# Seven-product pairs begun at pair 6 in the feed-forward entries, and conditioning units moved out of them

## The chip, the cores and the metric

The kernel runs on one core of a Trainium2 chip. The time is the device time of one execution in microseconds (us). Three runs of the kernel before gave 2658.09, 2658.15 and 2658.76 us (median 2658.15 us).

TensorE multiplies matrices and writes PSUM; VectorE (DVE in the rows) and ScalarE (ACT) do elementwise work; GpSimd (POOL) does elementwise work and issues some of the DMAs; the queue of SyncE (SP) issues the weight loads.

## The reference, cut to what matters

One inference step of a two-layer encoder over 576 tokens: 512 of a prompt and 64 of a sample, each group with a conditioning vector of its own. Per layer:

```
h += 1/2 * gate1 * RMSNorm(SwiGLU(mod1(RMSNorm(h))))     feed-forward "a"
x  = mod2(RMSNorm(h)); three mixers and a gated merge;  h += gate2 * RMSNorm(m @ W_out)
h += 1/2 * gate3 * RMSNorm(SwiGLU(mod3(RMSNorm(h))))     feed-forward "b"

swiglu(x, w1, w2): g, u = split(x @ w1); return (silu(g) * u) @ w2      x 576x1024, w1 1024x5504
mod, gate:         silu(c) @ w_ada + b_ada        9 vectors of 1024 for each layer and group
```

All of it is float32. The change touches the product `x @ w1` (four times: layers 0 and 1, "a" and "b") and the place in the program of a part of `silu(c) @ w_ada`.

## The kernel before, in words

**Products.** Activations lie transposed: features on the 128 partitions, the 576 tokens in two halves of 288 columns. Each float32 weight tile and each activation is split into a high part (a cast on ScalarE) and a low part (raw minus high, on VectorE), and a product is three matmuls: high x high, high weight x low activation, low weight x high activation. Weights come in chunks of 128x1024 in a ring of five slots (`SLOTS`), loaded by SyncE's queue when the chunk that had the slot five chunks earlier has been read (`load`). `split_hi` (line 1483) and `split_lo` (line 2004) make `w_hi` and `w_lo` of a chunk.

**A feed-forward entry.** The 5504 columns of `w1` are taken as 21 pairs (a gate tile and an up tile of 128 columns) and a half pair. A plain pair is two chunks, each 8 tiles x 3 matmuls x 2 halves, so 96 matmuls of 128x288. Pairs 0 to 4 (`NORMED = 5`) run on activations that lack the norm factor and the shift; beside them ScalarE and VectorE make the finished activation `x_full`, and the last of these pairs is followed by casting it into `x_hi` (line 1624) and subtracting to `x_lo` (line 2222). Pair 5 reads these tile by tile (`x_is_full`), pair 6 is plain too.

**Seven-product pairs.** Pairs 7 to 12 (`JOIN0, JOIN1 = 7, 13`) use Strassen's scheme in Winograd's form: gate and up tiles, the two halves of the rows and the two halves of the tokens make a 2x2 block product, done in seven block products instead of eight. That is 7 parts x 4 tiles x 3 = 84 matmuls of 128x288 (`joined_pair`; its matmuls are line 935). It needs sums of activations, `t_raw` (`t_sums`: four GpSimd instructions, lines 2911 to 2915, high parts at 1497, low parts at 2021), once for an entry, and sums of weights, `w_raw` (`sum_of_w`: four GpSimd instructions for a pair, called orders 0 to 3 here, line 2901; high parts 1492, low parts 2014), for each pair. TensorE reads a pair's weights as four chunks v = 0 to 3, and waits for the low part of each before parts 0, 2, 4 and 6. The low part of v = 0 stands behind order 1, those of v = 1, 2 and 3 behind order 3. VectorE adds the seven results up (line 2055).

Order 0 needs the loaded chunk v = 0, order 1 the chunk v = 1, order 2 the end of the chunk that holds the slot of v = 3, order 3 the chunk v = 2.

**Conditioning units.** A unit is one 128x512 piece of `w_ada`: a GpSimd-issued DMA into `ada_w`, and two VectorE instructions (line 2112) that multiply it by the conditioning of either group and sum along the row. `ADA_STAGES` says which stage computes which vectors, `f1_units`, `f2_units` and `gate_units` how many units VectorE does at each place. In layer 0's entry "a" alone, one unit stands in each seven-product pair, and GpSimd issues its next load between the pairs' weight sums.

The order of work on every engine is written out by hand. ScalarE, VectorE and GpSimd each run their list in that order.

Of the kernel before, what the change touches and what calls it, by code (L numbers as in the profile page):

```python
# [12 lines left out]
P = 128  # L13
# [3 lines left out]
TOK = SEQ + DEC  # L17
# [54 lines left out]
JOIN0, JOIN1 = 7, 13  # L72
# [19 lines left out]
ADA_STAGES = [((0, "f1a"), (2, 4, 3), (2, 4)), ((0, "f2a"), (3, 5, 7), (5, 7)), ((0, "gate"), (6,), (6,)),  # L92
# [37 lines left out]
def f1_units(l, ab, i):  # L130

    if (l, ab) == (1, "b"):
        return 2 if i >= JOIN1 else 0
    if (l, ab) == (0, "a"):
        return 1 if JOIN0 <= i < JOIN1 else {13: 5, 14: 5, 15: 6, 17: 5, 18: 5, 19: 4, 20: 4}.get(i, 0)
    return {13: 5, 14: 5, 15: 6, 17: 4, 18: 4, 19: 4, 20: 4}.get(i, 0)
# [20 lines left out]
def gate_units(m):  # L157

    return {1: (1, 1), 2: (1, 2), 3: (1, 2), 5: (1, 1), 6: (1, 2), 7: (1, 2)}.get(m, (0, 0))
# [258 lines left out]
def build_program(nc, ins, outs):  # L418
# [68 lines left out]
    ada_junk = sb("ada_junk", [P, ADA_K], at=big + JOIN1 * TOK * 4)  # L487
# [979 lines left out]
    def _(act):  # L1467
# [62 lines left out]
        def ffn_up(l, ab):  # L1530
# [12 lines left out]
            for i in range(NORMED):  # L1543
# [6 lines left out]
                else:  # L1550
                    for k in range(KD):
                        high_of_full(l, ab, k)
                        if k in (2, 5):
                            split_hi()
# [16 lines left out]
                elif i == 3:  # L1571
                    split_hi()
            for i in range(NORMED, KF - 1):
# [5 lines left out]
                if i == JOIN0 - 1:  # L1579
# [4 lines left out]
                if i == NORMED:  # L1584
                    high_of_t(l, ab, 2, 0)
                    high_of_t(l, ab, 1, 1)
                act.wait_ge(chunk_done.sem, chunk_done.done(0, chunk(l, ph, f1_chunk(i))))
                A(two(sil[:, i, :]), pair[0], ACT.Silu).then_inc(acc_free[0].sem, 1)
                if i == NORMED:
                    high_of_t(l, ab, 3, 2)  # L1590
                    high_of_t(l, ab, 0, 3)
                if i == JOIN0 - 1:
# [3 lines left out]
                if i > NORMED:  # L1596
                    split_hi()
# [385 lines left out]
    def _(dve):  # L1983
# [87 lines left out]
        def joined_stage(l, ab, i):  # L2071
# [22 lines left out]
            ada(l, "f1" + ab, f1_units(l, ab, i), ada_junk[:, :])  # L2094
# [7 lines left out]
        def ada(l, ph, n, junk=None):  # L2102

            for u in range(modulated[0], min(modulated[0] + n, ADA_ENDS[l, ph])):
# [4 lines left out]
                for g in (0, 1):  # L2109
                    so_far = ada_all[:, at, g:g + 1]  # L2110
                    out = ada_w[:, u % 2, :] if g else junk or ada_out[u % 2]
# [8 lines left out]
        def ffn_up(l, ab):  # L2120
# [4 lines left out]
            for i in range(NORMED):  # L2125
# [24 lines left out]
                else:  # L2150
                    for k in range(KD):
                        low_of_full(l, ab, k)
                        if k in (2, 5):
# [20 lines left out]
            for i in range(NORMED, KF - 1):  # L2174
# [3 lines left out]
                if i == NORMED:  # L2178
                    split_lo()
                    low_of_t(l, ab, 0)  # L2180
                    low_of_t(l, ab, 1)
                elif i == JOIN0 - 1:
                    low_of_t(l, ab, 2)
                    low_of_t(l, ab, 3)
                    low_of_joined(l, ab, JOIN0, 0)
# [10 lines left out]
                elif i > NORMED:  # L2196
# [571 lines left out]
        def merge(l):  # L2768
            for m in range(KD):
                g0, g1 = GROUP_AT["gate"]  # L2770
                for br, s in enumerate((0, 1, 0)):
                    if m or br == 2:
                        split_lo()
                    if br:
                        ada(l, "gate", gate_units(m)[br - 1])
# [87 lines left out]
    def _(pool):  # L2863
# [53 lines left out]
        def sums_and_loads(l, ab):  # L2917
# [249 lines left out]
```

## Time and profile before

| | |
|---|---|
| median of three runs | 2658.15 us |
| the profiled execution's own time | 2657.02 us |
| its span in the profile | 2655.3 us |
| TensorE busy | 2613.1 us, 98% of the span |
| VectorE busy | 1729.9 us, 65% |
| ScalarE busy | 1059.9 us, 40% |
| GpSimd busy | 393.8 us, 15% |
| granted TensorE clock, mean | 0.997 |

Busy times say how long an engine had work; a busy VectorE instruction can also be one that stands waiting inside itself, which only its length against others of its shape shows. The chain of waits is followed back from the last instruction, and shows which engine each stretch of time belongs to.

### The profile page before, as it was taken

Reading aid. Unit: us, or ns where it says so; the run is one execution under the profiler, and the core shown is the slowest. Engines: PE = TensorE matmul, PEld = TensorE weight load, DVE = VectorE, ACT = ScalarE, POOL = GpSimd, SP = SyncE. Lnnn points to the kernel's source line nnn. Section 1 sums busy time; section 2 is a strip of 40 time slices with the busy share of each in tenths; the row PEclk is TensorE's granted clock in tenths of the full one; section 3 lists DMA queues with packets and bytes.
Section 4 is the critical chain, followed back from the end, with each engine's and each line's share of the span. In section 5 each row is a group of like instructions: output and inputs, shape, how many; then the busy total and the mean of one; then the engine's idle time right before and its main releaser. Section 6 shows DMA issues by size and latency. Waiting matters only on the chain.

```text
span 2655.3 us, 49061 instructions
## 1 busy us (share of the span) xinstructions
PE 2613.1 (98%) x20410; PEld 2526.7 (95%) x20410; DVE 1729.9 (65%) x3490; ACT 1059.9 (40%) x1912; POOL 393.8 (15%) x484
## 2 busy tenths in 40 slices
PE   7999999999999999999999999999999999999997
PEld 6989999888999999999999999998889999999997
DVE  5797777766656487777487776576666565875423
ACT  4542224544422474322265322254452335542321
POOL 0341120110000013211104211101100000240000
PEclk9999999999999999999999999999999999999998
DMA  6245554443333323455423455534333332244321
GB/s 263 85 148 169 185 186 135 128 131 102 96 113 106 93 71 116 152 174 175 132 88 100 147 187 162 159 104 138 115 110 100 110 109 80 72 139 133 111 88 60
DMA packets 105997, 336.84 MB, mean 127 GB/s; under 512 B 15084, under 2 KB 18732, under 8 KB 105072
## 3 DMA queue, kind: packets, MB, share of 16 engines
q1 hardware_dynamic: 75376, 233.26, 27.0%
q0 software_dynamic: 30400, 100.45, 12.1%
q8 instruction: 161, 2.64, 0.4%
q14 instruction: 60, 0.49, 0.1%
HBM read 322.76 MB, written 11.55 MB: 126 GB/s over the span
## 4 chain that ended last, share of the span: by engine, by line
PE 92%; DVE 4%; issue 1%; DMA 1%; POOL 1%; ACT 0%; DVEq 0%; SPq 0%; ACTq 0%
PE ps L879 77%; PE ps L935 8%; PE ps L1318 2%; PE ps L1366 1%; PE ps L1342 1%; DMA ada_first<-in_ada_first 1%; DVE w_lo L2004 1%; PE ps L888 1%; POOL w_raw L2901 1%; DVE x_lo L2222 0%; DVE w_lo L2014 0%; PE ps L1335 0%; PE ps L997 0%; DVE hid L2161 0%; DVE prob L2677 0%
## 5 line engine op out<-in xcount | busy, mean ns | idle before, releaser
L879 PE MATMUL ps<-x_hi,w_hi 128*128 128x288 f32 (+1 forms) x3456 | 777.1, 299 | 4.3 <-DVE x_lo L2222 1.5
L879 PE MATMUL ps<-x_hi,w_lo 128*128 128x288 f32 (+1 forms) x3456 | 759.5, 294 | 0.0
L879 PE MATMUL ps<-x_lo,w_hi 128*128 128x288 f32 (+1 forms) x3456 | 759.5, 294 | 0.0
L879 PEld LDWEIGHTS ps<-x_hi,w_hi 128*128 128x128 f32 x3456 | 558.6, 188 | 18.0 <-issue 8.5
L879 PEld LDWEIGHTS ps<-x_lo,w_hi 128*128 128x128 f32 x3456 | 561.5, 188 | 0.3
L879 PEld LDWEIGHTS ps<-x_hi,w_lo 128*128 128x128 f32 x3456 | 561.5, 188 | 0.0
L2004 DVE TENSOR_TENSOR w_lo<-w_raw,w_hi 128x1024 fp32r<-128x1024 f32 x336 | 418.9, 1250 | 138.7 <-ACT w_hi L1483 136.2
L1483 ACT CAST w_hi<-w_raw 128x1024 fp32r<-128x1024 f32 x336 | 348.5, 1048 | 79.3 <-DMA w_raw<-in_f 78.6
L879 PE MATMUL ps<-hid_hi,w_hi 128*128 128x288 f32 x1344 | 301.1, 295 | 0.0
L879 PE MATMUL ps<-hid_lo,w_hi 128*128 128x288 f32 x1344 | 299.4, 293 | 0.0
L879 PE MATMUL ps<-hid_hi,w_lo 128*128 128x288 f32 x1344 | 299.0, 294 | 0.0
L2867 POOL DMA_DIRECT2D ada_w<-in_ada x256 | 137.9, 539 | 978.2 <-DVE ada_all L2112 965.4
L2112 DVE CUSTOM_DVE_ANT_0 ps<-ada_w,c_half,ada_all 128x512 f32<-128x512 f32 x250 | 189.0, 756 | 127.9 <-DMA ada_w<-in_ada 127.4
L879 PEld LDWEIGHTS ps<-hid_hi,w_hi 128*128 128x128 f32 x1344 | 219.8, 188 | 0.2
L879 PEld LDWEIGHTS ps<-hid_lo,w_hi 128*128 128x128 f32 x1344 | 219.4, 188 | 0.2
L879 PEld LDWEIGHTS ps<-hid_hi,w_lo 128*128 128x128 f32 x1344 | 217.2, 187 | 0.0
L2112 DVE CUSTOM_DVE_ANT_0 ada_w<-ada_w,c_half,ada_all 128x512 f32<-128x512 f32 x256 | 191.2, 747 | 0.0
L2901 POOL TENSOR_TENSOR w_raw<-w_raw 128x512 f32<-128x512 f32 x96 | 147.7, 1549 | 191.8 <-DMA w_raw<-in_f 113.5
L1656 ACT ACTIVATE sq<-ps 128x576 f32<-128x576 f32 x38 | 24.9, 655 | 294.5 <-PE ps L888 261.5
L2014 DVE TENSOR_TENSOR w_lo<-w_raw,w_hi 128x1024 fp32r<-128x1024 f32 x96 | 115.4, 1205 | 26.6 <-POOL w_raw L2901 26.6
L2243 DVE TENSOR_TENSOR acc_y<-acc_y,sq 128x576 f32<-128x576 f32 (+1 forms) x51 | 32.9, 644 | 142.5 <-ACT sq L1656 116.5
L1935 ACT ACTIVATE sig<-sig,z 128x512 f32<-128x512 f32 x96 | 46.0, 528 | 185.3 <-DVE z L2779 185.2
(279 smaller groups left out, 3805.5 us busy)
## 6 DMA issues: line engine op xcount, KB each, us to landing
w_raw<-in_f SPq DMA_DIRECT2D x236, 512.0 KB, 3.6
ada_w<-in_ada POOLq DMA_DIRECT2D x256, 256.0 KB, 3.3
w_raw<-in_gate SPq DMA_DIRECT2D x64, 512.0 KB, 3.7
w_raw<-in_f SPq DMA_DIRECT2D x92, 256.0 KB, 2.7
w_raw<-in_tri SPq DMA_DIRECT2D x40, 512.0 KB, 3.6
ada_first<-in_ada_first SPq DMA_DIRECT2D x4, 2048.0 KB, 21.3
w_raw<-in_wout SPq DMA_DIRECT2D x16, 512.0 KB, 3.6
c_half<-c_scratch POOLq DMA_DIRECT2D x12, 512.0 KB, 5.5
```

Source lines behind the costliest of these rows:

```text
L879: r = mm(ps[:, 2 * out + b, 0:width], w, xx[:, cols(b)], start=first and n == 0, stop=last and n == 2)
L888: r = mm(ps[:, 2 * out + b, 0:HALF], w[:, s, t * P:(t + 1) * P], hid_hi[:, k, columns(b)], start=False, stop=w is w_lo)
L935: r = mm(ps[:, bank, 0:HALF], w, moved, start=k == 0 and m == 0, stop=k == half_k - 1 and m == 2)
L1318: r = mm(out, q_st[rows, i * P:i * P + m], k, start=True, stop=True)
L1483: copy(w_hi[:, c % SLOTS, :], w_in[:, c % SLOTS, :]).then_inc(hi_ready.sem, 1)
L1935: r = A(sig[:, br, part], sig[:, br, part], ACT.Sigmoid, bias=c_col[:, br, g:g + 1])
L2004: V.tensor_tensor(w_lo[:, s, :], w_in[:, s, :], w_hi[:, s, :], ALU.subtract).then_inc(lo_ready.sem, 1)
L2014: V.tensor_tensor(w_lo[:, s, 0:n], w_in[:, s, 0:n], w_hi[:, s, 0:n], ALU.subtract).then_inc(lo_ready.sem, 1)
L2112: r = V.tensor_tensor_reduce(out, ada_w[:, u % 2, :], c_half[:, g, :], 1.0, so_far, ALU.mult, ALU.add, so_far)
L2243: V.tensor_tensor(total, total, more, ALU.add).then_inc(y_added.sem, 1)
L2867: nc.gpsimd.dma_start(dst, src).then_inc(signal.sem, 16)
L2901: nc.gpsimd.tensor_tensor(*operands, ALU.add).then_inc(w_sum.sem, 1)
```

## The change

Six edits:

1. The seven-product pairs begin at pair 6 instead of 7, in all four entries. Pair 5 is then the only plain pair between the making of `x_full` and the first seven-product pair.
2. ScalarE casts two of the four activation sums (`t_hi`) already after pair 3's work, ahead of the casts into `x_hi`, and the other two at the head of pair 5's work.
3. VectorE splits one weight chunk instead of two between its `x_lo` tiles, and does all four `t_lo` and the first pair's `w_lo` in pair 5's time.
4. No conditioning unit stands in a seven-product pair any more, and no load of one between weight sums. The scratch output `ada_junk` goes.
5. Layer 0's entry "a" has 32 units instead of 40 (all of them behind the seven-product pairs), its second stage 40 as before.
6. Layer 0's gate stage has 24 units instead of 16: four in each of six of its eight steps.

```diff
-JOIN0, JOIN1 = 7, 13
+JOIN0, JOIN1 = 6, 13
...
-ADA_STAGES = [((0, "f1a"), (2, 4, 3), (2, 4)), ((0, "f2a"), (3, 5, 7), (5, 7)), ((0, "gate"), (6,), (6,)),
+ADA_STAGES = [((0, "f1a"), (2, 4), (2, 4)), ((0, "f2a"), (3, 5, 7), (3, 5)), ((0, "gate"), (6, 7), (6,)),
...
-    if (l, ab) == (0, "a"):
-        return 1 if JOIN0 <= i < JOIN1 else {13: 5, 14: 5, 15: 6, 17: 5, 18: 5, 19: 4, 20: 4}.get(i, 0)
     return {13: 5, 14: 5, 15: 6, 17: 4, 18: 4, 19: 4, 20: 4}.get(i, 0)
...
-def gate_units(m):
+def gate_units(l, m):
+    if l == 0:
+        return {1: (2, 2), 2: (2, 2), 3: (2, 2), 4: (2, 2), 6: (2, 2), 7: (2, 2)}.get(m, (0, 0))
     return {1: (1, 1), 2: (1, 2), 3: (1, 2), 5: (1, 1), 6: (1, 2), 7: (1, 2)}.get(m, (0, 0))
...  ScalarE, ffn_up
                         high_of_full(l, ab, k)
-                        if k in (2, 5):
+                        if k == 3:
                             split_hi()
...
                 elif i == 3:
                     split_hi()
+                    high_of_t(l, ab, 2, 0)
+                    high_of_t(l, ab, 1, 1)
...
-                if i == JOIN0 - 1:
+                if i == NORMED:
+                    high_of_t(l, ab, 3, 2)
+                    high_of_t(l, ab, 0, 3)
                     high_of_joined(l, ab, JOIN0, 0)
                     high_of_joined(l, ab, JOIN0, 1)
...  VectorE, joined_stage and ffn_up
-            ada(l, "f1" + ab, f1_units(l, ab, i), ada_junk[:, :])
             product_of_joined(l, ab, i)
...
                         low_of_full(l, ab, k)
-                        if k in (2, 5):
+                        if k == 3:
                             split_lo()
...
                 if i == NORMED:
-                    split_lo()
                     low_of_t(l, ab, 0)
                     low_of_t(l, ab, 1)
-                elif i == JOIN0 - 1:
+                    low_of_joined(l, ab, JOIN0, 0)
                     low_of_t(l, ab, 2)
                     low_of_t(l, ab, 3)
-                    low_of_joined(l, ab, JOIN0, 0)
                     low_of_joined(l, ab, JOIN0, 1)
                     low_of_joined(l, ab, JOIN0, 2)
...  GpSimd, sums_and_loads
             ada_loads(l, ph, 0, 2)
-            at = 2
             t_sums(l, ab)
             for i in range(JOIN0, JOIN1):
-                if i > JOIN0 + 1 and f1_units(l, ab, i):
-                    ada_loads(l, ph, at, at + 1)
-                    at += 1
                 for order in range(4):
                     sum_of_w(l, ab, i, order)
-            ada_loads(l, ph, at)
+            ada_loads(l, ph, 2)
```

How the order on VectorE moves, at three places. In these rows `L2170` and the like are lines, `w_lo<-w_raw,w_hi` is the low part of a weight chunk, `x_lo` that of the finished activation, `t_lo` that of its sums, `hid_lo` that of a pair's result; the changed kernel's lines are 4 to 7 lower.

Place 1, VectorE between pair 3's result and the end of the finished activation's low parts, before:

```order
L2170 TENSOR_TENSOR hid_lo<-hid,hid_hi 128x576
L2004 TENSOR_TENSOR w_lo<-w_raw,w_hi 128x1024
L2222 TENSOR_TENSOR x_lo<-x_full,x_hi 128x2x288 x3
L2004 TENSOR_TENSOR w_lo<-w_raw,w_hi 128x1024
L2222 TENSOR_TENSOR x_lo<-x_full,x_hi 128x2x288 x3
L2004 TENSOR_TENSOR w_lo<-w_raw,w_hi 128x1024
L2222 TENSOR_TENSOR x_lo<-x_full,x_hi 128x2x288 x2
```

and now:

```order
L2165 TENSOR_TENSOR hid_lo<-hid,hid_hi 128x576
L2000 TENSOR_TENSOR w_lo<-w_raw,w_hi 128x1024
L2215 TENSOR_TENSOR x_lo<-x_full,x_hi 128x2x288 x4
L2000 TENSOR_TENSOR w_lo<-w_raw,w_hi 128x1024
L2215 TENSOR_TENSOR x_lo<-x_full,x_hi 128x2x288 x4
```

The chunk that was split between the sixth and seventh `x_lo` is gone from here (it was chunk 12, the first of pair 6).

Place 2, VectorE between pair 4's result and pair 6, before:

```order
L2170 TENSOR_TENSOR hid_lo<-hid,hid_hi 128x576
L2004 TENSOR_TENSOR w_lo<-w_raw,w_hi 128x1024
L2021 TENSOR_TENSOR t_lo<-t_raw,t_hi 128x1152 x2
L2193 TENSOR_TENSOR hid<-ps,sil 128x576
L2069 TENSOR_TENSOR hid_lo<-hid,hid_hi 128x576
L2021 TENSOR_TENSOR t_lo<-t_raw,t_hi 128x1152 x2
L2014 TENSOR_TENSOR w_lo<-w_raw,w_hi 128x1024 x3
L2193 TENSOR_TENSOR hid<-ps,sil 128x576
L2014 TENSOR_TENSOR w_lo<-w_raw,w_hi 128x512
```

and now:

```order
L2165 TENSOR_TENSOR hid_lo<-hid,hid_hi 128x576
L2017 TENSOR_TENSOR t_lo<-t_raw,t_hi 128x1152 x2
L2010 TENSOR_TENSOR w_lo<-w_raw,w_hi 128x1024
L2017 TENSOR_TENSOR t_lo<-t_raw,t_hi 128x1152 x2
L2010 TENSOR_TENSOR w_lo<-w_raw,w_hi 128x1024 x2
L2186 TENSOR_TENSOR hid<-ps,sil 128x576
L2010 TENSOR_TENSOR w_lo<-w_raw,w_hi 128x512
```

Four `t_lo` and two `w_lo` now stand ahead of part 2 of the first seven-product pair, all between pair 4's result and pair 5's; before, pair 5's result lay among them and a whole plain pair more of TensorE time.

Place 3, VectorE at the end of the first seven-product pair of layer 0's entry "a", before (the four `L2112` rows are one conditioning unit):

```order
L2014 TENSOR_TENSOR w_lo<-w_raw,w_hi 128x1024
L2112 ISA ada_junk,ada_all<-ada_w,c_half,ada_all 128x512
L2112 ISA ada_all 128x1
L2112 ISA ada_w,ada_all<-ada_w,c_half,ada_all 128x512
L2112 ISA ada_all 128x1
L2063 SCALAR_TENSOR_TENSOR hid<-hid,sil 128x576
L2014 TENSOR_TENSOR w_lo<-w_raw,w_hi 128x1024
```

and now:

```order
L2051 TENSOR_TENSOR sil<-sil,ps 128x288 x2
L2010 TENSOR_TENSOR w_lo<-w_raw,w_hi 128x1024
L2059 SCALAR_TENSOR_TENSOR hid<-hid,sil 128x576
L2010 TENSOR_TENSOR w_lo<-w_raw,w_hi 128x1024
L2065 TENSOR_TENSOR hid_lo<-hid,hid_hi 128x576
```

The unit is gone; the order is that of the other three entries. On GpSimd the 28 weight sums of this entry now stand in one row, with no load between them.

## Rows read from the trace of the kernel before

**Rows 1.** The page, busy time of each engine (span share, instructions).
```profile
PE 2613.1 (98%) x20410; PEld 2526.7 (95%) x20410; DVE 1729.9 (65%) x3490; ACT 1059.9 (40%) x1912; POOL 393.8 (15%) x484
```

**Rows 2.** Chain of waits, longest pieces: start us, us, what.
```profile
49.40 69.76 PE ps L879 x528
119.16 7.36 PE ps L935 x56
...
193.95 44.24 PE ps L879 x336
...
1001.51 20.81 PE ps L879 x156
1022.32 66.84 PE ps L935 x504
...
1428.35 66.88 PE ps L935 x504
```

**Rows 3.** Timeline of VectorE, layer 0 entry "a": start us, us, instruction.
```profile
132.70 0.74 DVE L2112 CUSTOM_DVE_ANT_0 ada_junk<-ada_w,c_half,ada_all 128x512 f32<-128x512 f32 x1
...
134.72 2.67 DVE L2014 TENSOR_TENSOR w_lo<-w_raw,w_hi 128x1024 fp32r<-128x1024 f32 x1
```

**Rows 4.** Stretch of layer 0's gate stage: us, busy of each engine.
```profile
737.00:762.00 25.00, 25.00 (x192) 25.00 (x191) 15.80 (x27) 7.33 (x11) 1.61 (x3) 1.00 0.37 117
```

**Rows 5.** Timeline of GpSimd, layer 0 entry "b".
```profile
984.50 3.11 POOL L2912 TENSOR_TENSOR t_raw<-x_full 128x1152 f32<-128x1152 f32 x1
987.57 5.85 POOL L2915 TENSOR_TENSOR t_raw<-t_raw,x_full 128x1152 f32<-128x1152 f32 x2
1001.57 1.72 POOL L2901 TENSOR_TENSOR w_raw<-w_raw 128x512 f32<-128x512 f32 x1 [8.15 <-DMA w_raw<-in_f]
1006.11 1.38 POOL L2901 TENSOR_TENSOR w_raw<-w_raw 128x512 f32<-128x512 f32 x1 [2.83 <-DMA w_raw<-in_f]
```

**Rows 6.** Timeline of VectorE, the same stretch.
```profile
984.24 3.45 DVE L2161 SCALAR_TENSOR_TENSOR hid<-hid,z,sil 128x512 f32<-128x512 f32 x2
988.43 2.44 DVE L2170 TENSOR_TENSOR hid_lo<-hid,hid_hi 128x576 fp32r<-128x576 f32 x1 [0.74 <-ACT hid_hi L1561]
990.80 3.71 DVE L2004 TENSOR_TENSOR w_lo<-w_raw,w_hi 128x1024 fp32r<-128x1024 f32 x1
994.43 2.08 DVE L2222 TENSOR_TENSOR x_lo<-x_full,x_hi 128x576 fp32r<-128x576 f32 x3
996.44 1.21 DVE L2004 TENSOR_TENSOR w_lo<-w_raw,w_hi 128x1024 fp32r<-128x1024 f32 x1
...
1002.05 0.74 DVE L2227 TENSOR_TENSOR sil<-ps,r 128x576 f32<-128x576 f32 x1
...
1003.89 0.95 DVE L2161 SCALAR_TENSOR_TENSOR hid<-hid,z,sil 128x512 f32<-128x512 f32 x2 [0.30 <-ACT sil L1557]
1005.58 0.76 DVE L2170 TENSOR_TENSOR hid_lo<-hid,hid_hi 128x576 fp32r<-128x576 f32 x1 [0.74 <-ACT hid_hi L1561]
1006.53 2.04 DVE L2004 TENSOR_TENSOR w_lo<-w_raw,w_hi 128x1024 fp32r<-128x1024 f32 x1 [0.19 <-ACT w_hi L1483]
...
1013.19 2.62 DVE L2021 TENSOR_TENSOR t_lo<-t_raw,t_hi 128x1152 fp32r<-128x1152 f32 x2
```

**Rows 7.** Issues on SyncE's DMA queue, the same stretch.
```profile
983.31 12.18 SPq L776 DMA_DIRECT2D w_raw<-in_f  x2
995.95 0.38 SPq L794 DMA_DIRECT2D w_raw<-in_f  x1
```

**Rows 8.** The page, DMA issues: KB each, median us from issue to landing.
```profile
w_raw<-in_f SPq DMA_DIRECT2D x236, 512.0 KB, 3.6
...
w_raw<-in_f SPq DMA_DIRECT2D x92, 256.0 KB, 2.7
```

**Rows 9.** Timeline of VectorE, layer 0 entry "a".
```profile
86.89 2.56 DVE L2170 TENSOR_TENSOR hid_lo<-hid,hid_hi 128x576 fp32r<-128x576 f32 x1 [0.74 <-ACT hid_hi L1561]
89.37 1.21 DVE L2004 TENSOR_TENSOR w_lo<-w_raw,w_hi 128x1024 fp32r<-128x1024 f32 x1
```

More of the change, by code:

```diff
@@ L486, in build_program @@
     t_hi = sb("t_hi", [P, 4, half_k, HALF], F32R, at=big + 14 * TOK * 4)
-    ada_junk = sb("ada_junk", [P, ADA_K], at=big + JOIN1 * TOK * 4)
     t_at = big + (KF + JOIN1) * TOK * 4
@@ L1583, in ffn_up @@
                     split_hi()
-                if i == NORMED:
-                    high_of_t(l, ab, 2, 0)
-                    high_of_t(l, ab, 1, 1)
                 act.wait_ge(chunk_done.sem, chunk_done.done(0, chunk(l, ph, f1_chunk(i))))
@@ L1589, in ffn_up @@
                 if i == NORMED:
-                    high_of_t(l, ab, 3, 2)
-                    high_of_t(l, ab, 0, 3)
-                if i == JOIN0 - 1:
                     high_of_joined(l, ab, JOIN0, 2)
@@ L1595, in ffn_up @@
                     continue
-                if i > NORMED:
-                    split_hi()
+                split_hi()
                 act.wait_ge(acc_free[1].sem, acc_free[1].done(l, GROUP_AT[ph][1] + f1_group(1, i)))
@@ L2100, in _, with ada @@
         modulated = [0]
-        def ada(l, ph, n, junk=None):
+        def ada(l, ph, n):
             for u in range(modulated[0], min(modulated[0] + n, ADA_ENDS[l, ph])):
@@ L2110, in ada @@
                     so_far = ada_all[:, at, g:g + 1]
-                    out = ada_w[:, u % 2, :] if g else junk or ada_out[u % 2]
+                    out = ada_w[:, u % 2, :] if g else ada_out[u % 2]
                     r = V.tensor_tensor_reduce(out, ada_w[:, u % 2, :], c_half[:, g, :], 1.0, so_far,
@@ L2195, in ffn_up @@
                     low_of_joined(l, ab, JOIN0, 3)
-                elif i > NORMED:
+                else:
                     split_lo()
@@ L2774, in merge @@
                     if br:
-                        ada(l, "gate", gate_units(m)[br - 1])
+                        ada(l, "gate", gate_units(l, m)[br - 1])
                     dve.wait_ge(chunk_done.sem, chunk_done.done(0, chunk(l, "gate", 4 * m + br)))
```

## The prediction

> **What bounds the kernel now.** I read the page's busy times first: TensorE is busy 2613.1 us, 98% of the span [rows 1]. So only two things can change the time much: fewer matmuls, or gaps between them. Next the chain of waits. In plain stretches a matmul of 128x288 costs 69.76 / 528 = 0.132 us [rows 2], so a plain pair costs 96 x 0.132 = 12.68 us. In layer 0's entry "b" the six seven-product pairs take 66.84 us for 504 matmuls, 11.14 us a pair, and in layer 1's "a" 66.88 us [rows 2]: TensorE never waits there. In layer 0's "a" they begin at 119.16 and the next plain stretch at 193.95 [rows 2]: 74.79 us, 12.47 a pair, so TensorE waits there for others. Last I read the timelines of VectorE, GpSimd and SyncE's queue just ahead of the first seven-product pair, since that is where one plain pair of TensorE time, the cover of the preparations, is taken away.
>
> **Matmuls saved.** One plain pair becomes a seven-product pair in each of four entries: 12.68 - 11.14 = 1.54 us each.
>
> **Units out of the seven-product pairs.** In layer 0's "a" VectorE's unit begins at 132.70 with two instructions of some 0.7 us, ahead of the pair's product, and the next weight split took 2.67 us [rows 3] where 1.21 is its usual length [rows 6]. Without units and without loads between the sums this entry has the instruction order of the others, so I take their 11.14 us. Pairs 6 to 12 cost 12.68 + 74.79 = 87.47 us now, and 7 x 11.14 = 77.98 then: 9.49 us less, if TensorE waits for nothing at the start. Bounds: 1.54 (the waits stay) and 9.49.
>
> **Eight more units in layer 0's gate stage.** In one of the stage's 25 us steps TensorE is busy 25.00, VectorE 15.80 with three units in it [rows 4]. A fourth adds 2 x 0.74 = 1.5 us, and its load goes beside. TensorE's full busy time hides it; cost 0. If the cover failed in all eight it would be 12 us, but VectorE has 9 us free in each step.
>
> **The cover that goes.** What is late is VectorE ahead of the first seven-product pair. The rows show a rule that decides it. Beside GpSimd's activation sums VectorE's instructions with both inputs in SBUF stretch: the result 3.45 us against 0.95, its low part 2.44 against 0.76, the weight split 3.71 against 1.21 [rows 6]; while instructions with one input in PSUM (0.74 at 1002.05, beside a weight sum at 1001.57) do not. The other way too: that weight sum took 1.72 against 1.29 while `x_lo` was running [rows 5]. The split at 1006.53 took 2.04: it stood until the sum at 1006.11 ended at 1007.49, and then ran 1.08. So the two engines exclude each other by whole instructions and alternate when both have work: where VectorE has a backlog, each GpSimd sum costs it 1.29 us. Before, only the sum at 1006.11 fell among such instructions of pairs 4 and 5; the sums of pair 7 had a plain pair more of time. Now I count, for layer 0's "b" (the profile's times):
>
> - VectorE is let go by the last activation sum at 987.57 + 5.85 = 993.42 [rows 5]. From there to the end of chunk 13's `w_lo` stands: rest of a split 1.07; eight `x_lo` at 0.67 = 5.36 (three take 994.43 to 996.44) and one split 1.13; 1.84 from the last `x_lo` to pair 4's result (1002.05 to 1003.89); 1.69 from there to its low part at 1005.58, and 0.68 for that; four `t_lo` at 1.27 = 5.08 (2.62 for two, with overlap); two splits 2.26 [rows 6]. Sum 19.1 us, so 1012.5.
> - When TensorE wants it: pair 4 ends at 995.95, when SyncE issues the next load [rows 7]; pair 5 takes 12.68, parts 0 and 1 of pair 6 take 2 x 12 x 0.1326 = 3.18: 1011.8. Without exclusion TensorE is 0.7 us late.
> - Added by exclusion: order 0 stands right behind the activation sums, since its chunk was asked for at 983.31 [rows 7]: 1.29. Order 1's load is issued at 995.1 (the second of two issues that end at 995.49 [rows 7]) and takes 2.7 [rows 8], so it falls at 998, among `x_lo`: 1.29. Orders 2 and 3 start when chunk 10 is read, some 0.4 us before pair 4's result: its two instructions each wait for one sum, partly inside the idle time: 1.9, between 1.3 and 2.6. Order 0 of pair 7 comes some 3.6 us after chunk 11 is read [rows 8], among the last two `t_lo`: 1.3, or 0 if late. Together 5.8, between 3.9 and 6.5.
>
> TensorE is then 6.5 us late at part 2: some 2.4 of it in pair 5 (waiting for `x_lo`, which the two first sums push to 1003.5), 2.3 before part 0, 1.8 before part 2. Now it is 1.0 late: 995.95 + 2 x 12.68 = 1021.3, and the first seven-product pair begins at 1022.32 [rows 2]. This entry: -1.54 + 6.5 - 1.0 = +4.0 us. Layer 1's entries have the same shape: together 3 x 4.0 = +12.0.
>
> Layer 0's "a": GpSimd is done at 89.45 - 0.68 = 88.8, which is 5.0 us before pair 4's end at 93.8 (below) where it is 2.5 in "b", and VectorE's split runs from 89.37 unhindered [rows 9]. 89.37 + 19.16 = 108.5; with order 0's 1.37 and the other 4.5, 114.4. TensorE's now unhindered pairs 5 and 6 start at 119.16 - 25.36 = 93.8, so part 2 wants it at 93.8 + 12.68 + 3.18 = 109.7: 4.7 late. This entry: -9.49 + 4.7 = -4.8.
>
> ScalarE is not late: its two early `t_hi` casts fit before VectorE takes up `x_lo`, and the last weight casts come just as VectorE wants them. Later parts are covered too: after part 2 the pair lasts 5 x 1.59 us more, in which VectorE has about 1 us to spare for pair 7's first split.
>
> **Sum:** -4.8 + 12.0 + 0 = +7.2 us on the execution's own 2657.02 (span 2655.3): 2664.2. The median of the runs lies 1.13 above that execution, so 2665. With the bounds of the exclusion (-1.9 to +0.7 for each of four entries): 2658 to 2668.
>
> **Rivals.**
>
> A: *the sums don't hold VectorE up*. Then stalls are 0 in layer 0's "a" and 0.7 in the others: -9.49 - 3 x (1.54 + 0.3) = -15.0, so 2643. For it: nothing but that each of VectorE's instructions could be long for another reason. Against it: the five stretched rows, each ending with a GpSimd sum.
> Here a page of the Trainium skill speaks against my sum: "Advanced Engine Details and Errata" (VectorE Performance Modes, mode summary) says that GpSimd interferes with VectorE's two-port modes, and these float32 two-input instructions run at no such rate; by it alone the sum would be rival A's. "SBUF — State Buffer" (Who interferes with whom) counts instructions with two SBUF inputs in, and gives the loser the wait for the whole instruction. The trace sides with the second: 3.71 us for 1.21 [rows 6].
>
> B: *the sums fall into VectorE's gaps*. If loads come later or sooner than I place them, half of the exclusion is hidden, 2.6 instead of 5.8. Stalls 1.5 and 3.3: -8.0 + 3 x 0.8 = -5.6, so 2652.5. For it: there are 0.74 and 0.30 us gaps and some 1.5 us of PSUM instructions. Against: VectorE is in backlog nearly throughout.
>
> C: *the backlog is carried into pair 7*. VectorE has about 1 us to spare before pair 7's first split; two more sums (1.29 each) in front of it make TensorE 1.6 us late again in each entry: +6.4, so 2671. It decides once more than one sum falls between part 2 and that split. The same time results if layer 0's "a" keeps 12 us a pair.
>
> The forecast is on the side of slower; A and B are the other side.
>
> **How the numbers follow.** Forecast 0.54, A 0.12, B 0.21, C 0.13. About 0.2% (5.3 us) is what a measurement of this kernel can tell from no change. The forecast's own range 2657 to 2669 puts two thirds of it over 2663.5 and one third within; B lies half within, half below 2652.8; A is below, C above. Slower 0.36 + 0.13 = 0.49; same 0.18 + 0.10 = 0.28; faster 0.12 + 0.11 = 0.23. The range that leaves 2 in 10 out: 2649 to 2671 (most of A is out, and a part of C).
>
> **What would show it.** Right: in the changed profile layer 0's "a" has some 78 us for seven pairs at 11.14 behind their start, without waits; in each entry TensorE waits for `x_lo` in pair 5 and for `w_lo` before part 0 and part 2 of pair 6; GpSimd's sums of pair 6 stand among `x_lo` and ahead of `t_lo`, each with a stretched VectorE instruction beside it; layer 0's gate stage keeps a full TensorE. Wrong: `x_lo` and `t_lo` at 0.67 and 1.27 us throughout, no wait at pair 6, or a gate stage with gaps; or 11.14 us not reached in layer 0's "a".

## The result and the profile after

| | before | after |
|---|---|---|
| median of 8 runs, us | 2658.64 | 2666.05 |
| lowest to highest | 2657.32 to 2659.12 | 2663.91 to 2667.14 |
| ratio, 95% interval | | 1.0027 (1.0017 to 1.0038) |
| profiled execution's span | 2655.3 | 2664.3 |

The changed kernel is 7.4 us slower by the medians, 0.3%; the forecast was +7.2 on the profiled execution and 2665 us. The profiled execution of before (2657.02) lay 1.6 us below the median of its runs, so the two spans differ by 9.0 us.

The page's busy times and GpSimd's, after (span share, instructions), answer to [rows 1]:

```profile
PE 2611.0 (98%) x20362; PEld 2523.2 (95%) x20362; DVE 1766.6 (66%) x3526; ACT 1067.0 (40%) x1924; POOL 418.4 (16%) x500
```

48 matmuls fewer (20410 to 20362), four times 12, and still a longer span. The longest pieces of the chain of waits after (start us, us, what), which answer to [rows 2]:

```profile
50.47 31.85 PE ps L878 x240
121.48 67.08 PE ps L934 x504
...
313.60 16.59 PE ps L878 x126
...
950.23 30.05 PE ps L878 x228
1014.87 75.06 PE ps L934 x564
...
1214.86 16.58 PE ps L878 x126
...
1360.37 30.05 PE ps L878 x228
...
1626.26 16.59 PE ps L878 x126
...
2260.57 30.05 PE ps L878 x228
...
2524.85 16.58 PE ps L878 x126
```

Before, the same marks stood at 49.40, 318.80, 953.25, 1213.72, 1359.28, 1620.14, 2254.84 and 2515.83. Subtracting neighbours gives the time of each stretch: each entry with the start of its second product, and what lies between.

| stretch, us | before | after | change | forecast |
|---|---|---|---|---|
| layer 0 "a" | 269.4 | 263.1 | -6.3 | -4.8 |
| layer 0 mixer and gate | 634.5 | 636.6 | +2.2 | 0 |
| layer 0 "b" | 260.5 | 264.6 | +4.2 | +4.0 |
| layer 1 "a" | 260.9 | 265.9 | +5.0 | +4.0 |
| layer 1 mixer and gate | 634.7 | 634.3 | -0.4 | 0 |
| layer 1 "b" | 261.0 | 264.3 | +3.3 | +4.0 |

The changes add up to +8.0, the forecasts to +7.2. What the table leaves out, the stretch between the layers and the end, is the same in both to 0.1 us. The program's start took 1.1 us more in this execution (the first mark, 50.47 for 49.40); that is not the change's.

What TensorE waited for, after (us in total, times, longest):

```profile
PE ps L934 <- DVE w_lo L2010: 12.5, 9, 2.2
...
PE ps L878 <- DVE x_lo L2215: 5.8, 6, 1.4
```

and the place of it, for which I take layer 0's "b". GpSimd's timeline after, which answers to [rows 5] (add 3.0 us to compare with times of before):

```profile
984.56 5.86 POOL L2908 TENSOR_TENSOR t_raw<-t_raw,x_full 128x1152 f32<-128x1152 f32 x2
990.36 2.28 POOL L2894 TENSOR_TENSOR w_raw<-w_raw 128x512 f32<-128x512 f32 x1
994.80 1.62 POOL L2894 TENSOR_TENSOR w_raw<-w_raw 128x512 f32<-128x512 f32 x1 [2.15 <-DMA w_raw<-in_f]
1001.80 3.00 POOL L2894 TENSOR_TENSOR w_raw<-w_raw 128x512 f32<-128x512 f32 x2 [5.38 <-PE ps L878]
1011.62 2.11 POOL L2894 TENSOR_TENSOR w_raw<-w_raw 128x512 f32<-128x512 f32 x1 [6.83 <-DMA w_raw<-in_f]
```

VectorE's timeline beside it, which answers to [rows 6]:

```profile
991.41 3.85 DVE L2215 TENSOR_TENSOR x_lo<-x_full,x_hi 128x576 fp32r<-128x576 f32 x4
995.19 2.31 DVE L2000 TENSOR_TENSOR w_lo<-w_raw,w_hi 128x1024 fp32r<-128x1024 f32 x1
997.43 2.75 DVE L2215 TENSOR_TENSOR x_lo<-x_full,x_hi 128x576 fp32r<-128x576 f32 x4
...
1001.95 2.94 DVE L2156 SCALAR_TENSOR_TENSOR hid<-hid,z,sil 128x512 f32<-128x512 f32 x2 [0.30 <-ACT sil L1556]
...
1012.51 3.45 DVE L2010 TENSOR_TENSOR w_lo<-w_raw,w_hi 128x1024 fp32r<-128x1024 f32 x2
```

Each of the five sums has a stretched VectorE instruction beside it: four `x_lo` in 3.85 us where the next four take 2.75; a split of 2.31 for 1.21; pair 4's result 2.94 for 0.95; two splits 3.45 for 2.35. The last `x_lo` ended at 1000.18 (forecast 1003.5 in times of before, 1000.5 here), chunk 13's low part at about 1014.9 (forecast 1018.3, here 1015.3), and TensorE goes on without a stop from 1014.87: 564 matmuls are all of the seven pairs but parts 0 and 1. Part 2 was due at 1008.8 (pair 4's end at 995.95 [rows 7], less the 3.0 us, plus 12.68 and 3.18), so TensorE was 6.1 us late; 6.5 was the forecast. Its waits here stand behind the first matmuls after them:

```profile
993.41 0.51 PE L878 MATMUL ps<-x_hi,w_hi 128*128 128x288 f32 x2 [0.51 <-DVE x_lo L2215]
998.23 0.54 PE L878 MATMUL ps<-x_hi,w_hi 128*128 128x288 f32 x2 [1.41 <-DVE x_lo L2215]
1010.20 0.37 PE L934 MATMUL ps<-x_hi,w_hi 128*128 128x288 f32 x1 [2.22 <-DVE w_lo L2010]
1014.87 0.40 PE L934 MATMUL ps<-t_hi,w_hi 128*128 128x288 f32 x1 [1.27 <-DVE w_lo L2010]
```

They are 1.9 us in pair 5, 2.2 before part 0 and 1.3 before part 2, where 2.4, 2.3 and 1.8 were forecast.

In layer 1's "b" the wait before part 2 is missing. There the granted clock of TensorE fell, right behind the 2.2 us wait before part 0. It was 0.50 (1.2 GHz) from 2321 to 2324 (us, busy us of TensorE, its weight loads, VectorE, ScalarE, GpSimd, then the clock):

```profile
2321.00:2324.00 3.00, 3.00 (x15) 3.00 (x14) 3.00 (x3) 1.19 (x3) 1.90 (x1) 0.50 0.15 58
```

The matmuls came 0.24 us apart there in place of 0.13. From part 0 to the end of the seven pairs took 79.74 us, as in layer 0's "b" with its wait before part 2 (1010.20 to 1089.93, 79.7), so here the lower clock took the place of that wait and cost next to nothing. Apart from this stretch and the last 15 us or so, which run at the lower clock in both kernels, the clock stood at 1.00 in both from 40 us on.

### The profile page after: what moved, and what is told of

Read it like the earlier page. It is cut to its first block, busy times and chain, and to the rows that moved or that the text cites. A ratio compares the mean times of both kernels' runs of the same rounds, so it can differ in the third digit from the quotient of the medians.

```text
span 2664.3 us, 49085 instructions
## 1 busy us (share of the span) xinstructions
PE 2611.0 (98%) x20362; PEld 2523.2 (95%) x20362; DVE 1766.6 (66%) x3526; ACT 1067.0 (40%) x1924; POOL 418.4 (16%) x500
## 4 chain that ended last, share of the span: by engine, by line
PE 87%; DVE 8%; ACT 2%; DMA 1%; issue 1%; DVEq 0%; SPq 0%; POOL 0%; ACTq 0%
PE ps L878 69%; PE ps L934 11%; PE ps L1317 2%; DVE w_lo L2000 1%; PE ps L1365 1%; PE ps L1341 1%; DVE hid L2156 1%; DVE x_lo L2215 1%; DVE ps L2107 1%; DMA ada_first<-in_ada_first 1%; DMA ada_w<-in_ada 1%; DVE ada_w L2107 1%; PE ps L887 1%; DVE w_lo L2010 1%; ACT w_hi L1482 1%
## 5 line engine op out<-in xcount | busy, mean ns | idle before, releaser
L878 PE MATMUL ps<-x_hi,w_hi 128*128 128x288 f32 (+1 forms) x3328 | 749.7, 299 | 8.6 <-DVE x_lo L2215 5.8
L878 PE MATMUL ps<-x_hi,w_lo 128*128 128x288 f32 (+1 forms) x3328 | 732.3, 294 | 0.0
L878 PE MATMUL ps<-x_lo,w_hi 128*128 128x288 f32 (+1 forms) x3328 | 732.2, 294 | 0.0
L878 PEld LDWEIGHTS ps<-x_hi,w_hi 128*128 128x128 f32 x3328 | 538.0, 188 | 22.3 <-issue 10.6
L878 PEld LDWEIGHTS ps<-x_lo,w_hi 128*128 128x128 f32 x3328 | 541.0, 188 | 0.3
L878 PEld LDWEIGHTS ps<-x_hi,w_lo 128*128 128x128 f32 x3328 | 541.2, 188 | 0.0
L2000 DVE TENSOR_TENSOR w_lo<-w_raw,w_hi 128x1024 fp32r<-128x1024 f32 x328 | 411.6, 1258 | 142.6 <-ACT w_hi L1482 139.6
L2894 POOL TENSOR_TENSOR w_raw<-w_raw 128x512 f32<-128x512 f32 x112 | 172.2, 1548 | 187.7 <-DMA w_raw<-in_f 112.5
L2010 DVE TENSOR_TENSOR w_lo<-w_raw,w_hi 128x1024 fp32r<-128x1024 f32 x112 | 136.7, 1224 | 22.6 <-POOL w_raw L2894 21.9
L934 PE MATMUL ps<-t_hi,w_hi 128*128 128x288 f32 x448 | 133.0, 297 | 2.7 <-DVE w_lo L2010 2.7
L934 PE MATMUL ps<-t_lo,w_hi 128*128 128x288 f32 x448 | 132.3, 295 | 0.0
```

Of the source, the lines that this page charges most:

```text
L878: r = mm(ps[:, 2 * out + b, 0:width], w, xx[:, cols(b)], start=first and n == 0, stop=last and n == 2)
L934: r = mm(ps[:, bank, 0:HALF], w, moved, start=k == 0 and m == 0, stop=k == half_k - 1 and m == 2)
L2000: V.tensor_tensor(w_lo[:, s, :], w_in[:, s, :], w_hi[:, s, :], ALU.subtract).then_inc(lo_ready.sem, 1)
L2010: V.tensor_tensor(w_lo[:, s, 0:n], w_in[:, s, 0:n], w_hi[:, s, 0:n], ALU.subtract).then_inc(lo_ready.sem, 1)
L2894: nc.gpsimd.tensor_tensor(*operands, ALU.add).then_inc(w_sum.sem, 1)
```

## The experiments

The numbers in brackets are the ratio to the kernel before and its 95% interval. The kernel before was timed again beside each group of experiments, with medians of 2658.43 us (experiments 1 to 4), 2658.75 (5 to 8) and 2658.07 (9 to 11). The changed kernel's 2666.05 is from its own eight runs, so differences of under 1 us between runs of different groups show nothing.

**1. The units alone.** The tables of the units as changed, in the kernel before:

```diff
-        return 1 if JOIN0 <= i < JOIN1 else {13: 5, 14: 5, 15: 6, 17: 5, 18: 5, 19: 4, 20: 4}.get(i, 0)
...
+        return {1: (2, 2), 2: (2, 2), 3: (2, 2), 4: (2, 2), 6: (2, 2), 7: (2, 2)}.get(m, (0, 0))
```

> The changed tables for the conditioning units alone (none in layer 0's seven-product pairs, four in six steps of its gate stage), with the seven-product pairs still beginning at pair 7 and the entries' old order. My theory: the units and their loads are what made layer 0's entry a take 12.47 us a pair, and the second unit in each gate slot lengthens a loop of VectorE and ScalarE to 6.69 us where TensorE needs 6.33. Then entry a falls from 74.8 to 66.9 us (-7.9), the gate stage gains 2.1: 2652.8 against 2658.6. Rival: what the first entry waits for is something of the program's start or of the loads, not the units: it stays over 72 us, and the time is 2658 to 2661.

Measured 2653.08 us (ratio 0.9981, 0.9972 to 0.9990). The chain of this kernel:

```profile
119.98 66.82 PE ps L935 x504
...
312.37 16.59 PE ps L879 x126
...
949.36 30.05 PE ps L879 x228
```

The six seven-product pairs of layer 0's "a" take 66.82 us, as forecast, where they took 74.79 [rows 2]. The stretch of the gate stage takes 949.36 - 312.37 = 637.0 us, 2.5 more than before. Both gain and loss are where the theory has them, and it stands.

**2. The first pair's weight sums as fills.** In the changed kernel:

```diff
+            if i == JOIN0:
+                nc.gpsimd.memset(operands[0], 0.0).then_inc(w_sum.sem, 1)
+                return
             nc.gpsimd.tensor_tensor(*operands, ALU.add).then_inc(w_sum.sem, 1)
```

> The changed kernel, where the four weight sums of the first seven-product pair of each entry are replaced by GpSimd fills with zero of the same places (they write as much and read nothing; the sums of that pair are left out of the computation). My theory: VectorE's instructions with two SBUF inputs and GpSimd's instructions that read SBUF exclude each other, and that is what makes TensorE wait at the first seven-product pair. Then x_lo, t_lo and w_lo run at 0.67, 1.27 and 1.13 us there, TensorE's waits shrink to under 1 us in layer 0's b and layer 1's entries and to none in layer 0's a: -17 to -22 us, 2644 to 2649. Rival: the loads, or ScalarE's casts, or the mere end of order 3 are what is late: the waits shrink only by what the fills are shorter, some 1 us an entry: about 2662.

Measured 2647.73 us (0.9961, 0.9947 to 0.9975): 18.3 less than the changed kernel. VectorE's timeline, layer 0's "b":

```profile
988.59 2.75 DVE L2215 TENSOR_TENSOR x_lo<-x_full,x_hi 128x576 fp32r<-128x576 f32 x4
991.27 1.21 DVE L2000 TENSOR_TENSOR w_lo<-w_raw,w_hi 128x1024 fp32r<-128x1024 f32 x1
...
996.92 0.95 DVE L2156 SCALAR_TENSOR_TENSOR hid<-hid,z,sil 128x512 f32<-128x512 f32 x2 [0.30 <-ACT sil L1556]
```

and what TensorE waited for in it:

```profile
PE ps L934 <- DVE w_lo L2010: 1.7, 9, 0.2
```

Loads and casts are the same; behind the activation sums the stretching is gone, and so are the waits for `x_lo` in pair 5 and nearly all of those for `w_lo` (12.5 us after the change). The rival fell. A fill also lasts only 0.52 us where a sum lasts 1.29, so this run alone doesn't say whether reading or duration matters; experiment 8 does.

**3. The gate stage in three slots.** In the changed kernel:

```diff
-                    if br:
-                        ada(l, "gate", gate_units(l, m)[br - 1])
+                    ada(l, "gate", gate_units(l, m)[br])          (1, 1, 2) for (2, 2)
```

> The changed kernel, where the four units in each of six steps of layer 0's gate stage stand as 1, 1 and 2 in three slots of the step in place of 2 and 2 in two. The same work in the stage. My theory: with two units in consecutive slots the loop take of a product, sigmoid and weight cast on ScalarE, low part and units on VectorE, next take lasts 6.69 us against TensorE's 6.33, so 2.1 us are lost over six steps: 2664.0 against 2666.1, with full TensorE slices in the stage. Rival: VectorE's load or the units' loads are what costs; then spreading changes nothing: 2666.

Measured 2662.75 us (1.0017, 1.0007 to 1.0026), 3.3 less than the changed kernel; the mixer and gate stretch took 634.5 us, as before the change (636.6 after), so 2.1 us of the gain lie in it, as forecast. The rest lies in the two "a" entries, 262.6 and 265.2 us for 263.1 and 265.9, and has no explanation here. The step of the stage after:

```profile
702.00:727.60 25.60, 25.50 (x193) 25.26 (x192) 17.30 (x32) 7.24 (x12) 2.16 (x4) 1.00 0.37 124
```

and with three slots (in both: us, then busy us of TensorE, its weight loads, VectorE, ScalarE, GpSimd):

```profile
700.00:725.00 25.00, 25.00 (x191) 25.00 (x190) 17.02 (x32) 7.33 (x11) 2.00 (x4) 1.00 0.40 127
```

VectorE's load is the same, with 8 us free; only the spacing differs. TensorE's busy time hardly shows the loss (25.50 of 25.60). The time from step to step does: the first sigmoids of two steps are 25.69 us apart after the change (701.85 to 727.54) and 25.37 with three slots (700.10 to 725.47). The loop shows on ScalarE, after the change:

```profile
701.85 0.96 ACT L1931 ACTIVATE sig<-sig,z 128x512 f32<-128x512 f32 x2 [3.75 <-DVE z L2772]
702.72 1.03 ACT L1482 CAST w_hi<-w_raw 128x1024 fp32r<-128x1024 f32 x1
708.53 0.96 ACT L1931 ACTIVATE sig<-sig,z 128x512 f32<-128x512 f32 x2 [4.78 <-DVE z L2772]
...
715.21 0.96 ACT L1931 ACTIVATE sig<-sig,z 128x512 f32<-128x512 f32 x2 [4.78 <-DVE z L2772]
```

The sigmoid comes every 6.68 us, where TensorE needs 48 x 0.132 = 6.33: VectorE's take (its reading of a finished product out of PSUM) starts the sigmoid, ScalarE's weight cast stands behind the sigmoid, VectorE's split and two units behind the cast, and the next take behind the units. One such slot costs nothing. With three slots one of them has two units as well, and its sigmoid also comes 6.68 us after the one before:

```profile
706.42 0.96 ACT L1931 ACTIVATE sig<-sig,z 128x512 f32<-128x512 f32 x2 [4.42 <-DVE z L2771]
713.10 0.96 ACT L1931 ACTIVATE sig<-sig,z 128x512 f32<-128x512 f32 x2 [4.78 <-DVE z L2771]
```

TensorE stays full there, and so it does in the kernel before, which has one such slot in a step (738.75 to 745.43). Two of them in a row are what TensorE has to wait for: after the change it began a pair of matmuls 0.53 us after the last in place of 0.26, at 715.23, when the second late take was done. The rival fell.

**4. Low parts in the order in which they are due.** In the changed kernel, VectorE (ScalarE's casts likewise):

```diff
+                    low_of_joined(l, ab, JOIN0, 0)
                     low_of_t(l, ab, 0)
                     low_of_t(l, ab, 1)
-                    low_of_joined(l, ab, JOIN0, 0)
+                    low_of_joined(l, ab, JOIN0, 1)
                     low_of_t(l, ab, 2)
                     low_of_t(l, ab, 3)
-                    low_of_joined(l, ab, JOIN0, 1)
```

> The changed kernel, where VectorE makes the low parts of the first seven-product pair in the order in which TensorE wants them: first weight chunk, activation sums 2 and 1, second weight chunk, sums 3 and 0, third chunk (ScalarE's casts likewise). Same work. My theory: TensorE's 2.3 us wait before part 0 goes (the first low part comes 2.5 us sooner) and most of the 1.8 before part 2; the wait for x_lo in pair 5 stays: -3 to -4 us an entry, 2650 to 2654. Rival: the backlog of VectorE, not its order, sets the first pair's end, and the waits move to parts 3 and 4: 2660 to 2666.

Measured 2668.12 us (1.0038, 1.0023 to 1.0053), not faster at all. My expectation was wrong. The rival was right that the waits move, and its time was 2 us too low. TensorE did start part 0 sooner, but so it was done with chunk 12 sooner, so the load for pair 7's second weight sum came sooner, and two sums, at 1014.31 and 1016.67, fell ahead of the third chunk's low part in place of one:

```profile
1013.94 3.71 DVE L2017 TENSOR_TENSOR t_lo<-t_raw,t_hi 128x1152 fp32r<-128x1152 f32 x2
1017.58 2.28 DVE L2010 TENSOR_TENSOR w_lo<-w_raw,w_hi 128x1024 fp32r<-128x1024 f32 x1
```

TensorE waited 2.37 us for that one, at part 4, until 1019.91. Moving the deadline moved the obstacle with it.

Part of the time is the clock's, which neither theory nor rival had in it. Behind this wait the granted clock fell, with TensorE busy throughout (the clock is 0.58 on average here, 0.50 at its lowest):

```profile
1019.90:1024.00 4.10, 4.09 (x19) 4.09 (x20) 3.75 (x8) 2.57 (x3) 0.00 (x0) 0.58 0.09 31
```

The 540 matmuls from 1019.91 on took 73.39 us; at the pace of the 564 after the change (75.06 us) they would have taken 71.9. The same happened in layer 0's "a" (73.38 us) and layer 1's "b" (73.32), so the lower clock cost some 4.5 us in all. Without it the profiled execution (2670.16 us) would have taken 2665.7 us, in the rival's range.

**5. The earlier beginning alone.** The changed kernel with the old tables of units, one in each of pairs 7 to 12 of layer 0's "a", and their loads between the weight sums as before (cut to one line):

```diff
+        return 1 if 7 <= i < JOIN1 else {13: 5, 14: 5, 15: 6, 17: 5, 18: 5, 19: 4, 20: 4}.get(i, 0)
```

> The seven-product pairs from pair 6 with the changed entries' order, but the conditioning units left as before: one in each of pairs 7 to 12 of layer 0's entry a, with its load between the weight sums, 16 in the gate stage. My theory: the earlier beginning costs by itself about +4 us in each of layer 0's b and layer 1's entries and about +2 in layer 0's a (where 7.9 us of waits on the units stay), the gate stage none: 2658.5 + 14 = 2672 to 2674. Rival: once TensorE waits at the first pair, the units' waits fall into the same gaps and cost nothing more: 2666 to 2668.

Measured 2673.06 us (1.0047, 1.0034 to 1.0061), as the theory had it; the rival fell. With experiment 1, medians against before: -5.4 for the units alone, +14.3 for the beginning alone, sum +8.9; both together +7.4. The 1.5 us between the two are not traced.

**6. Units out and the gate in three slots, pairs from 7.**

```diff
-        return {1: (2, 2), 2: (2, 2), 3: (2, 2), 4: (2, 2), 6: (2, 2), 7: (2, 2)}.get(m, (0, 0))
+        return (1, 1, 2) if m in (1, 2, 3, 4, 6, 7) else (0, 0, 0)
```

> The units out of the seven-product pairs, those pairs still from pair 7 as before the change, and the gate stage's four units a step as 1, 1 and 2 in three slots. My theory: the gains of the two parts add, since they lie in different stages: 2653.1 for the units alone, less 2.1 to 3 for the gate's loop: 2650 to 2651, faster than both kernels. Rival: the gate stage's gap is taken up later by a wait in the mixer or the out product: 2653.

Measured 2650.96 us (0.9966, 0.9953 to 0.9978): the two gains add. The mixer and gate stretch took 634.7 us, where it took 637.0 in experiment 1.

**7. The first activation sum sooner.** In the changed kernel, GpSimd:

```diff
-            pool.wait_ge(x_full_made.sem, x_full_made.done(l, (ab == "b") * KD + KD - 1))
+            pool.wait_ge(x_full_made.sem, x_full_made.done(l, (ab == "b") * KD + KD // 2 - 1))
...
             nc.gpsimd.tensor_tensor(t_raw[:, 0, :, :], x00, x01, ALU.subtract).then_inc(t_sum.sem, 1)
+            pool.wait_ge(x_full_made.sem, x_full_made.done(l, (ab == "b") * KD + KD - 1))
```

> The changed kernel, where GpSimd makes the first of the four activation sums as soon as the first half of the finished activation is there, in place of waiting for all of it. Same work. My theory: GpSimd is done with these sums 2.7 us sooner, VectorE's backlog begins 2.7 us sooner, and TensorE is 2.5 us less late at part 2 of pair 6 in each entry: -8 to -10 us, 2656 to 2658. Rival: the loads or ScalarE set the end of the first pair's preparation: 2665 to 2666. A second rival: the early sum blocks VectorE where it was just in time, and costs there what it gives here: 2663 to 2666.

Measured 2663.27 us, 2.8 less than the changed kernel, a third of what I expected. The chain of this kernel shows why:

```profile
971.42 2.70 DVE hid L2156 x2
974.14 0.68 ACT hid_hi L1560
974.81 0.95 ACT w_hi L1482
975.76 4.16 ACT x_full L1608 x8
```

The early sum held pair 2's result (2.70 us for 0.95), the rest of `x_full` stands behind that result on ScalarE, and the other three sums behind `x_full`. From the end of TensorE's product of pair 3 to the end of the sums took 8.8 us (979.70 to 988.52) in place of 10.1 (980.28 to 990.42): 1.3 us sooner, where 2.7 were expected. Half of the gain was paid there, as the second rival had it, and the time lies in that rival's range.

**8. The activation sums as fills.** In the changed kernel, all four like this:

```diff
-            nc.gpsimd.tensor_tensor(t_raw[:, 0, :, :], x00, x01, ALU.subtract).then_inc(t_sum.sem, 1)
+            nc.gpsimd.memset(t_raw[:, 0, :, :], 0.0).then_inc(t_sum.sem, 1)
```

> The changed kernel, where GpSimd's four activation sums are fills with zero (they read nothing; these sums are left out of the computation), and the weight sums stay. My theory: VectorE is held up by what reads SBUF on GpSimd, whichever sums these are: pair 3's result, its low part and the next weight split take 0.95, 0.76 and 1.21 us in place of 3.45, 2.44 and 3.71, VectorE's backlog begins some 5 us sooner and the weight sums' 5.8 us still leave TensorE about 1 to 2 us late: -16 to -20, 2646 to 2650. Rival: only the weight sums matter, since they lie among the low parts that TensorE waits for: 2664 to 2666.

Measured 2643.10 us, 22.9 less than the changed kernel, more than expected. GpSimd's fills in layer 0's "b":

```profile
976.37 1.06 POOL L2905 MEMSET t_raw<- 128x1152 f32 x1
977.38 2.18 POOL L2908 MEMSET t_raw<- 128x1152 f32 x2
```

and VectorE in the same time:

```profile
977.79 0.95 DVE L2156 SCALAR_TENSOR_TENSOR hid<-hid,z,sil 128x512 f32<-128x512 f32 x2
```

The fills ran until 979.56, all through the result, and it took its usual 0.95 us. So it is not any GpSimd instruction that holds VectorE up: a fill, which reads nothing, does not, and a sum, which reads SBUF, does. The weight sums, left in, still stretch `t_lo` here (3.72 us for 2.62), but VectorE's backlog begins so much sooner that no wait of TensorE for `x_lo` or for the low parts of a seven-product pair is left in the list. I had expected 1 to 2 us of them in each entry.

**9. The first pair's weight sums as fills, pairs from 7.** Experiment 2's edit in experiment 1's kernel.

> The kernel with the units out of the seven-product pairs and these pairs still from pair 7, where the four weight sums of the first seven-product pair are fills with zero (these sums are left out of the computation). My theory: a plain pair more of TensorE's time covers all that GpSimd's sums cost VectorE, so taking the cost away gives little: 2650.5 to 2653.1, at most 2.5 us (the 1 us wait in pair 5 in three entries) against 18.4 us for the same fills with the pairs from 6. Rival: a weight sum costs the end its 1.3 us wherever it stands: 2640 to 2645.

Measured 2652.64 us (0.9980, 0.9970 to 0.9989) against 2653.08 with the sums: no change. The same fills gave 18.3 us with the pairs from 6. The sums do cost VectorE something with the pairs from 7, though less: in experiment 1's layer 0 "b" one split took 2.05 us for 1.21 (1002.62), and VectorE then stood 2.42 us until the last two sums of the pair were done (1015.47). TensorE waited for none of it. The plain pair of TensorE time spreads the sums out and covers what they cost.

**10. A weight split behind the eighth `x_lo`.** In the changed kernel (ScalarE likewise):

```diff
-                        if k == 3:
+                        if k == KD - 1:
                             split_lo()
```

> The changed kernel, where the weight chunk that VectorE splits between the fourth and fifth low part of the finished activation is split behind the eighth (ScalarE's cast too). Same work. My theory: TensorE waits some 1.1 us less in pair 5, and as much more at pair 6, since VectorE's backlog ends at the same time: no change, 2665 to 2667. Rival: the wait in pair 5 is a loss of its own: 2662 to 2663.

Measured 2661.93 us (1.0012, 1.0003 to 1.0021), 4.1 less than the changed kernel; I had expected no change. TensorE reads chunk 10 sooner, so orders 2 and 3 start sooner, and the first of them falls into the time of VectorE's PSUM instructions:

```profile
1000.40 2.55 POOL L2894 TENSOR_TENSOR w_raw<-w_raw 128x512 f32<-128x512 f32 x2 [4.24 <-PE ps L878]
```

Pair 4's result, at 1001.70, took 2.00 us in place of 2.94: the backlog itself had become 0.9 us shorter. Part 0 of pair 6 began as much sooner: 59.0 us behind the start of the entry's second product, where it was 60.0. The time is the rival's to 0.1 us, but by the rival TensorE would have gained the 1.1 us that it waited less in pair 5. The three later entries took 263.7, 264.1 and 263.3 us, 0.9, 1.8 and 0.9 less than after the change; layer 0's "a" took the same.

**11. The best version.** Experiment 6 with experiment 7's edit.

> The best version so far (units out of the seven-product pairs, these from pair 7, gate units in three slots) with GpSimd's first activation sum made as soon as half of the finished activation is there. My theory: as in the changed kernel the sums end 1.3 us sooner, and TensorE's wait of about 1 us in pair 5 goes in three entries: 2648 to 2649.5. Rival: that wait is not set by the sums' end: 2651; or the early sum holds up pair 2's result and the finished activation more than it gives: 2652 or more.

Measured 2649.29 us (0.9969, 0.9957 to 0.9980). It beats both kernels. TensorE's waits for `x_lo` in pair 5 fell from 1.5 us in all (experiment 6) to 0.7. The medians of the two experiments are 1.7 us apart, but their runs overlap (2648.14 to 2651.83 and 2650.23 to 2652.01), and against the kernel before, as timed beside each, their ratios are the same within the intervals: that this version is faster than experiment 6 is not shown.

## Why the prediction was right

- **Matmuls saved and the steady pace.** Right: the last six pairs of layer 0's "a" take 67.08 us, 11.18 each, and experiment 1 gave the units' 8.0 us to 0.1. The first of the seven took 12.9 us (108.60 to 121.48), which belongs to the cover.
- **The cover that goes.** Right in mechanism, place and size: +4.0 was forecast for each of three entries, +4.2, +5.0 and +3.3 came, and the waits stand where they were forecast. In layer 0's "b" TensorE was 6.1 us late at part 2, which by the forecast's sum (-1.54 + 6.1 - 1.0) makes +3.5; the other 0.6 us came behind it and are not traced. Experiment 9 against 2 shows that it is the cover, experiment 8 that fills, which read nothing, do not hold VectorE up where sums do. The page of the Trainium skill "SBUF — State Buffer" (Who interferes with whom) has just this condition, two SBUF inputs against a GpSimd instruction that reads; rival A, with the rule of the other page, fell.
- **Layer 0's "a"** gained 1.5 us more than forecast, and not by the forecast's sum. Part 2 of pair 6 began 1.4 us late (112.18; due at 109.7, plus the 1.1 us of the start), where 4.7 was forecast. Two terms of 1.3 us each were not paid there. One is order 1's: the sum came while `x_lo` was running and waited for them:

```profile
97.01 3.39 POOL L2894 TENSOR_TENSOR w_raw<-w_raw 128x512 f32<-128x512 f32 x1 [5.34 <-DMA w_raw<-in_f]
```

  3.39 us for 1.29, beside four `x_lo` in 2.75, unstretched. It then ran beside PSUM instructions and cost nothing. This is luck: the same sum, coming at nearly the same point of the first `x_lo`, was kept out in experiment 3 as well (3.50 us) and let in at once in experiments 4 and 5 (1.46 us). The other is that of pair 7's first sum, at 111.19, which ran only after the low part that part 2 needs:

```profile
110.91 3.43 DVE L2010 TENSOR_TENSOR w_lo<-w_raw,w_hi 128x1024 fp32r<-128x1024 f32 x2
```

  Against that, TensorE waited again where the forecast had "Later parts are covered too", for pair 7's first low part:

```profile
121.48 0.37 PE L934 MATMUL ps<-x_hi,w_hi 128*128 128x288 f32 x1 [1.09 <-DVE w_lo L2010]
```

  The seven pairs ended 6.5 us sooner than before, out of the 9.49 possible: 3.0 us were lost, of which 1.4 ahead of part 2.
- **The gate stage** is where the prediction had a step wrong: "TensorE's full busy time hides it; cost 0". It cost 2.2 us, since free time of VectorE in a step says nothing about two slots in a row with a loop of 6.68 us through two engines. Experiment 3 took it away.
- **Layer 1's "a"** took 1 us more than forecast, with a wait of TensorE of 1.08 us at 1467.80, before the first part of a later pair; the chain leads back from it to a pair of weight sums at 1454.11. With the wait at 121.48 in layer 0's "a" it is the only one inside the later pairs. Both look like rival C in small, but no run isolated it.
- **Rivals B and C.** B (half of the exclusion hidden) was not the case in the three later entries, though layer 0's "a" reached part 2 as B had it (1.4 us late; B: 1.5). Experiment 10 shows how near B lies: a pair of sums that began 1.2 us sooner is worth 0.9 us an entry. Experiment 4 has C's mechanism one place earlier: one more sum ahead of a low part of pair 6, and a second wait.
- **The clock** is in no term of the forecast, and the trace before gave no reason for one: the longest wait in these pairs was 1.0 us. After the change it fell once, where it cost next to nothing; in experiment 4 it cost some 4.5 us. So the price of a wait in this kernel is not only its length, and that it cost so little in the changed kernel is luck.
- The total was right partly by luck, since the two largest misses, -1.5 and +2.2, nearly cancel.

## What to carry to other kernels

A transformation that saves 1.5 us of matmuls each time can be worth less than the plain work that covers its preparation: before starting it sooner, sum up what the other engines must finish in the time that is left, with the time for which they exclude each other. Where a stage has a full TensorE and a VectorE that is a third idle, also sum up the loop of waits through the other engines in one slot; work that fits the average may not fit the loop in several slots on end, and spreading it over the slots cost nothing here. When two edits come together, time each alone: here one was worth -5 and the other +14.

## What the runs showed of the hardware

- GpSimd fills of SBUF (128x1152, 1.06 us) ran beside a VectorE instruction with two SBUF inputs and left it at 0.95 us (experiment 8); GpSimd sums of the same shape (2.7 us) stretched the same one to 3.45.
- A waiting GpSimd sum is not let in at every boundary between VectorE instructions: four `x_lo` of 0.67 us each kept one out for 2.1 us (layer 0's "a" after the change). Others were let in at a boundary with a weight split, and in experiment 10 one at 994.36 between two `x_lo` (1.80 us). What decides is not shown.
- Behind a wait of TensorE of 2.2 to 2.4 us at the first seven-product pair its granted clock fell to 0.50 (1.2 GHz) for some 3.5 us in some entries (one after the change, three in experiment 4), while TensorE was busy, and stayed at 1.00 behind waits of the same length in others (2.22 us in layer 0's "b" and in layer 1's "a" after the change). What decides is not shown. In the kernel before, where no wait in these pairs is over 1.0 us, it fell in none of them.
